# The shift, scale and gate totals of an adaLN modulation: shift and scale end as columns, and the bias is added in the totals

## The reference

```python
def modulated_sublayer(x, mod, g_pre, g_post, fn, weight):
    shift, scale, gate = mod[:, 0], mod[:, 1], mod[:, 2]
    h = rmsnorm(x, g_pre) * (1.0 + scale) + shift
    y = rmsnorm(fn(h), g_post)
    return x + weight * (1.0 + gate) * y
...
    sc = jax.nn.silu(c)
    for i in range(DEPTH):
        mod = (sc @ ada_w[i] + ada_b[i]).reshape(B, N_MOD, D_MODEL)[:, :, None, :]
```

## Time and profile before

| | |
|---|---|
| median of 3 runs | 1854.14 us (1851.59 to 1854.83) |
| profiled execution | 1848.86 us |
| its span, first to last instruction | 1847.0 us |
| mean granted clock of PE | 0.955 |
| PE busy | 1700.0 us, 92% |
| DVE busy | 1092.1 us, 59% |
| ACT busy | 874.4 us, 47% |

### The profile page before, as it was taken

One profiled execution on the slowest core, in us unless ns is written; L12 is line 12 of the kernel. 1 busy time (PEld: TensorE's weight loads), 2 busy tenths in 40 slices (PEclk: granted clock), 3 DMA queues, 4 the chain that ended last, 5 costly groups with the idle time before them and its releaser, 6 DMA issues.

```text
span 1847.0 us, 19745 instructions
## 1 busy us (share of the span) xinstructions
PE 1700.0 (92%) x7873; PEld 1289.2 (70%) x7873; DVE 1092.1 (59%) x1531; ACT 874.4 (47%) x1256; POOL 19.6 (1%) x39
## 2 busy tenths in 40 slices
PE   5999999899998999979899997999888778999997
PEld 1676766476776778856668886876667667777875
DVE  2545446564455545553555555577676647988886
ACT  2444333243344434435544444454544436767774
POOL 1000000000000000000000000000000000000000
PEclk9999999799999999999899999999789889999999
DMA  9777665646785585543265654444023136989993
GB/s 357 274 265 259 228 234 210 240 160 228 261 284 179 174 287 187 178 149 137 69 215 175 198 187 103 162 143 157 26 91 103 46 99 229 362 304 337 323 326 146
DMA packets 211313, 373.76 MB, mean 202 GB/s; under 512 B 8880, under 2 KB 102486, under 8 KB 211216
## 3 DMA queue, kind: packets, MB, share of 16 engines
q1 hardware_dynamic: 208368, 364.52, 57.8%
q0 software_dynamic: 2448, 6.82, 1.4%
q10 hardware_dynamic: 400, 1.10, 0.2%
HBM read 371.36 MB, written 1.05 MB: 202 GB/s over the span
## 4 chain that ended last, share of the span: by engine, by line
PE 82%; DVE 9%; ACT 5%; DMA 3%; issue 1%; SPq 0%; DVEq 0%; ACTq 0%
PE banks L516 22%; PE banks L518 21%; PE banks L517 21%; PE banks L557 2%; DVE ul L460 2%; PE banks L692 2%; DMA raw<-in_ada_w 2%; PE banks L577 1%; DMA raw<-in_ffn_w_in 1%; PE banks L550 1%; ACT uh L449 1%; PE banks L1200 1%; PE banks L1653 1%; ACT full L664 1%; PE banks L1173 1%; PE banks L2102 1%
## 5 line engine op out<-in xcount | busy, mean ns | idle before, releaser
L460 DVE TENSOR_TENSOR ul<-raw,uh 128x1024 fp32r<-128x1024 f32 (+2 forms) x548 | 659.8, 1212 | 449.8 <-ACT uh L449 441.8
L449 ACT ACTIVATE uh<-raw 128x1024 fp32r<-128x1024 f32 (+2 forms) x548 | 570.2, 1048 | 488.6 <-PE banks L518 376.9
L516 PE MATMUL banks<-uh,hh 128*128 128x512 f32 (+2 forms) x1280 | 528.0, 413 | 14.5 <-DVE hl L729 5.9
L518 PE MATMUL banks<-uh,hl 128*128 128x512 f32 (+2 forms) x1280 | 503.1, 393 | 0.0
L517 PE MATMUL banks<-ul,hh 128*128 128x512 f32 (+2 forms) x1280 | 502.1, 392 | 0.0
L516 PEld LDWEIGHTS banks<-uh,hh 128*128 128x128 f32 x1280 | 245.4, 192 | 93.5 <-issue 27.4
L517 PEld LDWEIGHTS banks<-ul,hh 128*128 128x128 f32 x1280 | 245.8, 192 | 53.3 <-issue 7.7
L518 PEld LDWEIGHTS banks<-uh,hl 128*128 128x128 f32 x1280 | 245.0, 191 | 52.1
L516 PE MATMUL banks<-uh,bh 128*128 128x512 f32 x528 | 211.8, 401 | 16.1 <-DVE bl L858 8.1
L518 PE MATMUL banks<-uh,bl 128*128 128x512 f32 x528 | 207.6, 393 | 0.0
L517 PE MATMUL banks<-ul,bh 128*128 128x512 f32 x528 | 207.2, 392 | 0.0
(11 more groups left out here) (300 smaller groups left out, 1332.1 us busy)
## 6 DMA issues: line engine op xcount, KB each, us to landing
raw<-in_ffn_w_in SPq DMA_DIRECT2D x176, 512.0 KB, 6.2
raw<-in_ada_w SPq DMA_DIRECT2D x72, 1024.0 KB, 7.0
raw<-in_w_up SPq DMA_DIRECT2D x64, 1024.0 KB, 5.6
raw<-in_ffn_w_out SPq DMA_DIRECT2D x44, 1024.0 KB, 9.8
raw<-in_w_down SPq DMA_DIRECT2D x32, 1024.0 KB, 5.6
raw<-in_w_in SPq DMA_DIRECT2D x22, 1024.0 KB, 5.1
raw<-in_w_mem_kv SPq DMA_DIRECT2D x4, 1024.0 KB, 10.3
raw<-in_mla_w_o SPq DMA_DIRECT2D x4, 1024.0 KB, 5.0
```

The lines of the kernel that those rows point to most:

```text
L449: act.e.activation(uh[r][:, 0:w], raw[m % NRAW][:, h * w:(h + 1) * w], AF.Copy).then_inc(act_done, ta.put("hi", u))
L460: dve.e.tensor_tensor(ul[r][:, 0:w], raw[m % NRAW][:, h * w:(h + 1) * w], uh[r][:, 0:w].bitcast(F32), ALU.subtract).then_inc(dve_done, tv. ...
L516: pe.e.matmul(o, a, wh, start=s0, stop=False)
L518: mm = pe.e.matmul(o, b, wh, start=False, stop=s1)
```

## The change

The bias product leaves the parts. The eight products of a piece now go to groups 0, 1, 2, 3, 0, 1, 2, 3, the first four of them as the start of their group. The totals get a common function, `ada_sum_pe`. For a gate it is the sum as before and the bias as a second product of 36 rows, 128 wide and 512 long, into the same bank. For shift and scale it is, for each of the four blocks of 128 channels, a product with the block of the copied buffer as the stationary and one column of `sum4` as the moving operand, and another with the block of `adab` as the stationary and one column of `ident`; both go to one column of the bank. DVE then reads four columns: a copy for the shift, one combined step with `ngc` for the scale. The product with the identity and the reduce are gone. Waits for `ident` and `ada_b` move along with the bias.

```diff
@@ -541,21 +541,15 @@
 
 
         def ada_parts_pe(pe, a, b):
-            i, j = a
-            r = i * 18 + j
-            got = [take_raw(pe, ("ada", i, j)) for _ in range(2)]
-            pe.wait_ge(loaded("ident"), 16)
-            pe.wait_ge(loaded("ada_b"), 16)
+            got = [take_raw(pe, ("ada",) + a) for _ in range(2)]
             pe.take(b)
-            pe.e.matmul(PB[b][0:32, :], ident[0:36, r:r + 1].to_broadcast([36, 32]), adab[0:36, :],
-                        start=True, stop=False)
             pe.wait_ge(act_done, ta("sc"))
             for k in range(KD):
                 m, w = got[k // 4]
-                g = (k + 1) % 4
+                g = k % 4
                 pe.wait_ge(ring[m % NRAW], landed[m])
                 mm = pe.e.matmul(PB[b][32 * g:32 * g + 32, :], sc[:, k:k + 1].to_broadcast([P, 32]), w[:, k % 4, :],
-                                 start=(k < 3), stop=(k >= 4))
+                                 start=(k < 4), stop=(k >= 4))
                 if k % 4 == 3:
                     mm.then_inc(pe_done, tp.put("raw", m))
             tp.same("ada_p", a)
@@ -570,36 +564,49 @@
             act.own()
             act.e.activation(buf, PB[b], AF.Copy).then_inc(act_done, ta.put("ada_c", a))
 
+        def ada_place(a):
+            i, j = a
+            return i * 18 + j, i * 3 + j // 6, (j // 2) % 3, j % 2
+
+        def ada_sum_pe(pe, a, b, part, pick):
+
+
+            r, s, kind, half = ada_place(a)
+            pe.wait_ge(loaded("ident"), 16)
+            pe.wait_ge(loaded("ada_b"), 16)
+            pe.take(b)
+            if kind == 2:
+                pe.e.matmul(PB[b], pick, part, start=True, stop=False)
+                mm = pe.e.matmul(PB[b], ident[0:36, r:r + 1].to_broadcast([36, P]), adab[0:36, :], start=False,
+                                 stop=True)
+            else:
+                for k in range(4):
+                    o = PB[b][:, k:k + 1]
+                    pe.e.matmul(o, part[:, k * P:(k + 1) * P], pick[:, 0:1], start=True, stop=False)
+                    mm = pe.e.matmul(o, adab[0:36, k * P:(k + 1) * P], ident[0:36, r:r + 1], start=False, stop=True)
+            mm.then_inc(pe_done, tp.put("ada_t", a))
+            pe.frees(b, dve_done, tv, "ada_e", a)
+
         def ada_total_pe(pe, a, b, buf):
             pe.wait_ge(act_done, ta("ada_c", a))
             pe.wait_ge(loaded("sum4"), 16)
-            pe.take(b)
-            pe.e.matmul(PB[b], sum4[:, :], buf, start=True, stop=True).then_inc(pe_done, tp.put("ada_t", a))
-            pe.frees(b, dve_done, tv, "ada_e", a)
+            ada_sum_pe(pe, a, b, buf, sum4[:, :])
 
         def ada_end_dve(dve, a, b):
-            i, j = a
-            s, kind, half = i * 3 + j // 6, (j // 2) % 3, j % 2
+            r, s, kind, half = ada_place(a)
             dve.wait_ge(pe_done, tp("ada_t", a))
+            dst = None if kind == 2 else ab[:, s, 1 - kind, half * 4:half * 4 + 4]
             if kind == 2:
                 g = G[s % 3][:, half * 512:half * 512 + 512]
                 dve.wait_ge(loaded(f"G{s}"), 16)
-                dve.e.scalar_tensor_tensor(g, PB[b], 1.0, g, ALU.add, ALU.mult).then_inc(
-                    dve_done, tv.put("ada_e", a))
-                return
-            d = full[:, 1, :].rearrange("p (a b) -> p a b", b=P)
-            dst = ab[:, s, 1 - kind, half * 4:half * 4 + 4]
-            dve.own()
-            dve.e.tensor_tensor(d, PB[b].rearrange("p (a b) -> p a b", b=P),
-                                ident[:, :].unsqueeze(1).to_broadcast([P, 4, P]), ALU.mult).then_inc(
-                dve_done, tv.put())
-            dve.own()
-            dve.e.tensor_reduce(dst, d, AX_X, ALU.add).then_inc(dve_done, tv.put())
-            if kind == 1:
-                gc_ = ngc[:, i * 48 + (s % 3) * 16 + half * 4:i * 48 + (s % 3) * 16 + half * 4 + 4]
+                end = dve.e.scalar_tensor_tensor(g, PB[b], 1.0, g, ALU.add, ALU.mult)
+            elif kind == 1:
+                c0 = a[0] * 48 + (s % 3) * 16 + half * 4
                 dve.own()
-                dve.e.scalar_tensor_tensor(dst, dst, 1.0, gc_, ALU.add, ALU.mult).then_inc(dve_done, tv.put())
-            tv.same("ada_e", a)
+                end = dve.e.scalar_tensor_tensor(dst, PB[b][:, 0:4], 1.0, ngc[:, c0:c0 + 4], ALU.add, ALU.mult)
+            else:
+                end = dve.e.tensor_copy(dst, PB[b][:, 0:4])
+            end.then_inc(dve_done, tv.put("ada_e", a))
 
         def total_step_pe(pe, w, a, b, buf):
             yield w
```

## The result

The changed kernel takes **1911.84 us** (median of 4 runs, 1908.76 to 1912.24) against 1854.49 us of the kernel before in the same comparison: a ratio of **1.0304, 95% interval 1.0282 to 1.0326**, 57 us more. Its profiled execution took 1911.62 us, 62.8 more than the one that the prediction was made against.

The account below looks back on a forecast made before the run. The prediction took TensorE to bound the kernel. Its terms summed to +25.4 us, with clock falls (+14.4 and +3.5) to +43.3 on 1848.9: 1892 us profiled, 1897 as median, range 1865 to 1918.

Parts of the forecast that it names:

- The bias leaves the parts: Modulation pieces on TensorE: dropping the two-pass bias product saves 0.97 us each where TensorE sets the time, -19.4 us.
- Gate totals: Twelve gate pieces: the bias product in the total adds 1.26 us each, ten on TensorE's path, +12.6 us.
- Column totals of 2.5 us: Shift and scale totals: 16 passes in blocks of 0.31 us, 1.64 us more each, +29.5 us for 18 dense ones.
- The attention wait: Attention part: the second total's 1.70 us wait for VectorE shrinks to some 0.4, -1.3 us.
- Pool: Pool, where the chain runs over TensorE: fewer biases against dearer totals and gates, +0.7 us.
- Start: Kernel start: four column totals on TensorE outlast the work VectorE loses, +2.9 us, and +3.5 for the clock.
- The clock: Behind dense column totals: quiet lowers TensorE's clock after nine of 18, 1.6 us each, +14.4 us.
- Rival A: Same costs on TensorE as the forecast, but the clock holds; 1880 us, chance 0.21.
- B: Column totals: changes of form cost nothing for one-column products, or these run in one pass; 1857 or 1859 us, chance 0.12.
- C: Column totals: loads vanish behind each other, leaving only VectorE's relief and the bias; 1823 us, chance 0.04.
- D: Column totals: blocks at the 0.42 us upper bound and a clock fall after nearly every total; 1929 us, chance 0.05.

Follow-up runs that it names:

- padded: The changed kernel with the bias tile zero-filled to 128 rows, so bias products have as many rows as the sums; 1869.04 us, ratio 1.0094.
- sums-first kernel: The changed kernel with the same products reordered in a column total, four sums and then four biases; 1881.91 us, ratio 1.0171.
- Filler ahead of them: The changed kernel with the four old bias products issued again at the start, into a bank nobody reads; 1901.02 us, ratio 1.0258.
- kernel with halves: The changed kernel with column totals behind feed-forward blocks cut into two halves, at least one weight unit between them; 1898.30 us, ratio 1.0244.
- second profile: The changed kernel run once more, unaltered, for another profile; 1910.03 us (one run).
- kernel with columns alone: Against the changed kernel, bias back in the parts; shift and scale totals are four one-column products, VectorE's relief stays; 1853.35 us, ratio 1.0001.
- first profile of before: The unchanged kernel's profiled execution that the prediction started from, 1848.9 us; its second profile, the same kernel once more, measured 1859.28 us.
- all totals as rows: Against the changed kernel, bias still in the totals, but every total a row of 512 columns and VectorE working as before; 1884.17 us, ratio 1.0182.

## Why the prediction came out as it did

The forecast was 1897 us in a range of 1865 to 1918, by its likeliest case; measured 1911.8. The mechanism held: changes of form and falls of the clock on TensorE's path. Three terms were too small: the number of falls, the start and the pool. By its steps:

1. *The bias leaves the parts, -0.97 each:* right. 2.83 to 1.89 us at the first piece, 2.82 to 1.86 at the second (82.96 to 85.78 before, 93.32 to 95.18 after).
2. *Gate totals, +1.26:* right. From 0.86 to 2.11 in a dense row, +1.25.
3. *Column totals of 2.5 us in blocks of 0.31:* right. The block is exact, and the total adds 2.48 us to a dense row where 0.86 stood, +1.62 against the 1.64 put. Right too is the working behind it, 0.20 for a change with the first load in it and 0.11 for the second pass: the padded and the sums-first kernel, 1.70 and 1.85 us a total, leave 0.07 to 0.10 for the change itself. The rule that one column costs as much as 60 (the Trainium skill, TensorEngine Tiling (Array Packing), Instruction Overhead) would have a total of 16 passes done in an estimated 0.4 us: the trace does not agree, not even without changes of form (1.70 us). The Trainium skill's remark that a change of tiling mode drains the engine (TensorEngine Tiling (Array Packing), Key Properties) fits the cost of the changes, though 36 rows against 128 was not shown to be such a change.
4. *The attention wait, -1.3:* right by itself (1.70 to 0.25). What stands behind it failed: at 961.56 the second total runs at half clock.
5. *Pool, +0.7:* mis-sized. VectorE is held for 3.1 us longer, since the clock fell in the middle of the three totals (0.50 from 353.6 on) and the last gate total took 4.00 us where 2.00 are usual.
6. *Start, +2.9, and +3.5 for the clock:* measured +10.1. I had read the clock as full at 36 us, as it was before, and put its fall within the totals. Here no rise came ahead of them, and all four ran at 0.51 a block: 16.4 us instead of 10. Filler ahead of them bought only 1.7 us.
7. *The clock, nine falls at 1.6, +14.4:* the price of one is right, their number not. Between the first and the last piece of the first feed-forward lie 10 pieces' parts, 4 gate and 6 column totals: -9.7 + 4 x 1.25 + 6 x 1.62 = +5.0 us. Two waits of 2.15 us in all vanish, so +2.9; the kernel with halves, without a fall, has +2.2. The change has +10.4, so against the halves its five falls there cost 8.2 us, 1.6 each; the three of the second profile cost 5.1, 1.7 each. The second feed-forward repeats it (+2.5 with halves, +4.2 with the change). Over all, 13 totals have a fall behind them, four more than put; in the pool, at the attention and behind waits of VectorE existing falls also became longer. Between 72 and 988 us the change spends 55 us more at half clock, by an estimate from the 1.6 us of a fall some 26 us of time where 14.4 stood.

One thing the prediction did not see at all went the other way: the wait at 182.98 is set by a transfer. It had taken any delay up to its own length for nothing, and would have eaten any gain, as the kernel with columns alone shows. There is luck in how near the total came. With the measured sizes in place of the three small terms the sum would be some 60 us, and 50.5 were measured in these stages. Waits that took up cost ahead of them, which the sum leaves out, make up for a part of the difference: 2.15 us in the first feed-forward alone. Part may be half clock that fell in waits, which the 26 us count as work; no run shows how much.

Up to the attention the sum was 43 us; measured are 50.5 against the first profile of before, 49.2 against the second. The other 12.3 us of the profiled execution lie where the change has no part; two executions of the kernel before differ there by 9.2. Of the 57 us between the medians some 7 are left that I can't place to a stage: both profiles of the change took 922 us at the end, those of before 910 and 919. Whether the change makes that end slower in the mean stays open; the kernels with columns alone and with all totals as rows took 919 and 920 us there, the change with filler 912.6.

Rival A (the clock holds) was wrong by these falls, B by the changes of form, C by the length of the totals. D had the block too dear and a fall behind nearly every total; of its two parts the clock was the nearer one.

## What to carry to other kernels

A product of one column is paid by its load (0.11 us a pass here) and by the change of row count ahead of it (0.07 to 0.10), so products with the same number of rows belong together, and one that adds a small bias belongs where a wide product stands anyway or, better, off TensorE. Count the time in which TensorE only loads and streams single columns: at 0.8 to 1.1 us a fall of the clock came once in 60 cases, at 2.4 us in six of ten, and a fall costs 1.6 us, about as much as 16 such passes. Before counting on a gain ahead of a wait, see what ends the wait: where it is a transfer, the gain stops there.

## What the runs showed of the hardware

- The row count of the stationary matters by itself: 16 passes of one column take 1.70 us all on 128 rows, 1.85 with one switch from 128 to 36, 2.38 with seven.
- At half clock a total of 2.38 us takes 4.11 (four in 16.43), less than twice, but all of it on the path. Without changes of form a pass takes 0.21 us in place of 0.11 (64 passes in 13.74 us at the start of the padded kernel).
- Behind totals of single columns, the clock falls even with TensorE busy without a gap: its busy share was 220.70 of 220.70 us in the first feed-forward. Busy by the records is not what holds the clock.
- The scatter of this kernel between runs (1846 to 1863 us) goes with the mean granted clock (0.956 to 0.947), and in the two profiles of before it lies almost whole in the end behind 937 us, where waits are many.
